# A chunked recurrence on one NeuronCore: scores by quarter array and masked by chunk instead of whole 128-squares

## What is computed

```
def step(S, inp):
    r_t, k_t, v_t, w_t, kk_t, a_t = inp
    sa = einsum('bhvk,bhk->bhv', S, -kk_t)
    S = S * w_t + sa[..., None] * (kk_t * a_t) + v_t[..., None] * k_t
    y = einsum('bhvk,bhk->bhv', S, r_t)
    return S, y
_, y = lax.scan(step, S0, xs)          # 1024 steps, one state per head
```

## Time and profile before

| what | value |
|---|---|
| median of the three timed executions | 2477.08 us |
| the three | 2471.67, 2477.08, 2477.37 us |
| the profiled execution: its own time | 2472.17 us |
| its span, first to last instruction | 2470.4 us |
| mean granted TensorE clock | 0.995 |
| groups in the recurrence | 16 (4 pairs of 4) |
| from one group's first score matmul to the next one's | 39.8 us |

### The profile page before, as it was taken

One profiled execution on the slowest core, in us unless ns is written; L12 is line 12 of the kernel. 1 busy time (PEld: TensorE's weight loads), 2 busy tenths in 40 slices (PEclk: granted clock), 3 DMA queues, 4 the chain that ended last, 5 costly groups with the idle time before them and its releaser, 6 DMA issues.

```text
span 2470.4 us, 33707 instructions
## 1 busy us (share of the span) xinstructions
PE 2376.4 (96%) x12944; PEld 1918.5 (78%) x12944; DVE 1303.9 (53%) x1480; ACT 697.3 (28%) x1103; POOL 773.1 (31%) x416
## 2 busy tenths in 40 slices
PE   5999999999999999998999999999999999999997
PEld 3788878887887788787877788888878787777775
DVE  6553353426342643565638744554451287757766
ACT  3412222223221321433215211111122454214441
POOL 1311131123112313112455433333334445422154
PEclk9999999999999999999999999999999999999998
DMA  3211111121112113663443311111114343211123
GB/s 120 69 52 52 70 51 52 52 69 51 53 50 69 51 52 116 204 203 127 172 150 122 101 42 51 43 50 43 50 53 135 126 120 104 73 61 36 35 77 111
DMA packets 61904, 205.22 MB, mean 83 GB/s; under 512 B 6240, under 2 KB 10464, under 8 KB 61152
## 3 DMA queue, kind: packets, MB, share of 16 engines
q1 hardware_dynamic: 40560, 138.76, 18.0%
q10 hardware_dynamic: 21232, 64.80, 7.2%
HBM read 167.36 MB, written 36.18 MB: 82 GB/s over the span
## 4 chain that ended last, share of the span: by engine, by line
PE 81%; DVE 11%; ACT 3%; DVEq 3%; issue 2%; ACTq 0%; DMA 0%; POOL 0%; POOLq 0%
PE psg L458 9%; PE psg L454 9%; PE psg L459 9%; PE psg L587 5%; PE psg L585 5%; PE psg L580 5%; PE psa L677 1%; PE psg L1125 1%; PE psg L1118 1%; PE psg L1123 1%; PE psb L666 1%; PE psg L1168 1%; PE psg L1162 1%; PE psg L1166 1%; PE psb L673 1%
## 5 line engine op out<-in xcount | busy, mean ns | idle before, releaser
L390 POOL CAST whi<-wraw 128x1024 fp32r<-128x1024 f32 (+1 forms) x176 | 183.1, 1040 | 1471.5 <-PE psg L580 558.2
L392 POOL TENSOR_TENSOR wlo<-wraw,whi 128x1024 fp32r<-128x1024 f32 (+1 forms) x176 | 461.4, 2621 | 27.4 <-issue 6.3
L458 PE MATMUL psg<-xlo,whi 128*128 128x512 f32 x1008 | 400.9, 398 | 0.0
L454 PE MATMUL psg<-xhi,whi 128*128 128x512 f32 x1008 | 398.3, 395 | 2.2 <-issue 1.8
L459 PE MATMUL psg<-xhi,wlo 128*128 128x512 f32 x1008 | 396.9, 394 | 0.0
L585 PE MATMUL psg<-xlo,whi 128*128 128x512 f32 x640 | 260.4, 407 | 0.0
L587 PE MATMUL psg<-xhi,wlo 128*128 128x512 f32 x640 | 260.2, 407 | 0.0
L580 PE MATMUL psg<-xhi,whi 128*128 128x512 f32 x640 | 258.1, 403 | 0.0
L454 PEld LDWEIGHTS psg<-xhi,whi 128*128 128x128 f32 x1008 | 189.2, 188 | 51.9 <-issue 3.2
L458 PEld LDWEIGHTS psg<-xlo,whi 128*128 128x128 f32 x1008 | 189.2, 188 | 45.4 <-issue 0.7
L459 PEld LDWEIGHTS psg<-xhi,wlo 128*128 128x128 f32 x1008 | 189.2, 188 | 44.8
(11 more groups left out here) (595 smaller groups left out, 4815.0 us busy)
## 6 DMA issues: line engine op xcount, KB each, us to landing
wraw<-w SPq DMA_DIRECT2D x224, 512.0 KB, 3.5
later_scratch<-stage ACTq DMA_DIRECT2D x40, 512.0 KB, 2.6
xres<-xt ACTq DMA_DIRECT2D x4, 1024.0 KB, 10.8
RV<-later_scratch SPq DMA_DIRECT2D x4, 1024.0 KB, 12.0
RG<-later_scratch SPq DMA_DIRECT2D x4, 1024.0 KB, 6.3
later_scratch<-rstage ACTq DMA_DIRECT2D x8, 512.0 KB, 2.6
mgr<-later_scratch ACTq DMA_DIRECT2D x8, 512.0 KB, 3.6
mgt<-later_scratch ACTq DMA_DIRECT2D x8, 512.0 KB, 4.6
```

What stands on the lines that cost most here:

```text
L390: pool.tensor_copy(whi[:, u, 0:width], wraw[:, u, 0:width])
L392: pool.tensor_tensor(wlo[:, u, 0:width], wraw[:, u, 0:width], whi[:, u, 0:width].bitcast(F32), ALU.subtract).then_inc(w_ready, 1)
L454: mm = pe.matmul(ps[:, cols], whi[:, slot, w_cols], rhs_hi(k, cols), start=(k == 0), stop=False)
L458: pe.matmul(ps[:, cols], whi[:, slot, w_cols], rhs_lo(k, cols), start=False, stop=False)
```

## The change

The scores are computed by chunk. For each square and each of the two key tiles, four matmuls with 64 rows (head h), 64 weight columns (the keys of chunk c) and 128 streamed columns (the same chunk c of the two query-side tiles) write to partitions 64c to 64c+63 of the head's bank. Head and chunk together choose a quarter of the 128x128 array. The order of the quarters is (0,0), (1,1), (0,1), (1,0), first for `KK`, then for `K`; `scores` is raised by the last two of each square. The off-diagonal blocks are not computed. The mask multiplications are done by chunk as well, two of 64x256 in place of one of 128x512, and no longer write the off-diagonal blocks, which stay as they were set at the beginning. The first group also increments `go` after its wait.

```diff
+        HALVES = [slice(c * CH, c * CH + CH) for c in range(2)]
...
                 pe.wait_ge(sem("rw_prep"), i + 1)
+                pe.sem_inc(go, 1)
                 for g in range(GROUPS):
...
                     for tt in range(2):
                         tl = 2 * g + tt
-                        for h in range(2):
-                            rows = slice(h * CH, h * CH + CH)
-                            kr = KR[rows, tl, :, :].rearrange("p a b -> p (a b)")
-                            pe.matmul(bank[2 * tt + h][:, 0:256], KK[rows, tl * P:tl * P + P], kr,
-                                      start=True, stop=True)
-                            pe.matmul(bank[2 * tt + h][:, 256:512], K[rows, tl * P:tl * P + P], kr,
-                                      start=True, stop=True).then_inc(sem("scores"), 1)
+                        for src, first in ((KK, 0), (K, 256)):
+                            for h, c in ((0, 0), (1, 1), (0, 1), (1, 0)):
+                                rows, chunk = HALVES[h], HALVES[c]
+                                out = bank[2 * tt + h][chunk, first:first + 256].rearrange("p (a b) -> p a b", a=2)
+                                mm = pe.matmul(out[:, :, chunk], src[rows, tl * P + c * CH:tl * P + c * CH + CH],
+                                               KR[rows, tl, :, chunk], start=True, stop=True)
+                                if first and h != c:
+                                    mm.then_inc(sem("scores"), 1)
...
-                    msk = mat[:, M_STRICT:M_STRICT + 2, :].rearrange("p a b -> p (a b)").unsqueeze(1
-                                                                                    ).broadcast_to([P, 2, 256])
                     for q in range(4):
                         v.wait_ge(sem("scores"), 16 * i + 4 * g + q + 1)
-                        tt(SC[:, q, :].rearrange("p (a x) -> p a x", a=2)[:, :, 0:256],
-                           bank[q].rearrange("p (a x) -> p a x", a=2), msk, MUL).then_inc(sem("sc_out"), 1)
+                        for chunk in HALVES:
+                            msk = mat[chunk, M_STRICT:M_STRICT + 2, chunk].unsqueeze(1).broadcast_to([CH, 2, 2, CH])
+                            mm = tt(SC[chunk, q, :].rearrange("p (a x b) -> p a x b", a=2, b=P)[:, :, 0:2, chunk],
+                                    bank[q][chunk, :].rearrange("p (a x b) -> p a x b", a=2, x=2)[:, :, :, chunk],
+                                    msk, MUL)
+                        mm.then_inc(sem("sc_out"), 1)
```

## The result

| | before | changed |
|---|---|---|
| median | 2474.32 us (5 executions, 2471.67 to 2477.37) | 2485.45 us (5 executions, 2483.79 to 2487.33) |
| profiled execution | 2472.17 us | 2487.33 us |
| one group's first score to the next one's | 39.80 us | 40.51 us |
| first score to L653 (now L657) | 6.62 us | 7.33 us |

The ratio of the changed kernel to the one before is 1.0045, with a 95% interval of 1.0034 to 1.0056: slower by 0.45%, or 11.1 us between the medians. The forecast was 2486, a loss of 9.4 us against a kernel before of 2477; with all five executions counted that kernel stands at 2474.32.

What follows compares the result with a forecast made beforehand. The chain scores, VectorE masks, L1404, copies, ScalarE, L653 was taken to bound each group. 16 x (0.99 - 0.42) + 0.3 = 9.4 us on a median of 2477.1 gave 2486 us, range 2474 to 2494.

Steps and rivals of the forecast that it cites:

- Scores, four quarters at once: Score matmuls on TensorE: all four quarters run together, first mask's operand complete after 0.70 us; gain 0.42 us a group.
- The rival of two at a time: Score matmuls: only two quarters run at a time, gain 0.01 us a group; 2493 us, chance 0.18.
- Masks: VectorE: eight half masks at 0.435 us each, 3.48 instead of 2.49; cost 0.99 us a group.
- The overlap rival: VectorE: changing halves does not hold half masks, chain changes by -0.04 us a group; 2477 us, chance 0.10.
- reckoned break-even: Half masks on VectorE: at steps of 0.356 us the chain is as long as before, below it faster.
- It, the copies and ScalarE are unchanged: Chain after the last mask: L1404 still comes 0.09 us later; it, the copies and ScalarE cost nothing extra.
- The limit of 0.38 a group: At L653: fills would let it start only 0.38 us earlier; used in the faster rival, 2471 us, chance 0.04.
- The increment of `go`: Extra semaphore step once a pair, at TensorE's wait for L1395: 0 to 0.1 us each, 0.3 us taken in all.
- A slip in the chances: Chance that the time stays the same, within 0.3%: summed from 0.15 + 0.10 + 0.02, given as 0.26.
- costed nothing for the clock: TensorE's new idle stretches stay well below the 1.5 us at L629, where mean granted clock was 0.995; no cost.

Runs made afterwards that it cites:

- the control: The kernel before with one fill matmul moved from level 1 to ahead of L653; median 2471.33 us, ratio 0.9984.

## Why the prediction was right

**The reading that carried it** was that VectorE's chain and not TensorE's work sets a group. The two half changes show it in both directions: the scores alone give 0.44 a group, the masks alone take 1.17, and in all six kernels without moved fills the period is the time from first score to L653 plus 33.17 to 33.19.

**How much of the hit is luck.** The forecast of 2486 lies 0.5 us from the measured 2485.45, closer than its terms. Its loss was 1.7 us too small (9.4 against 11.1), and the median that it started from 2.8 too high (2477.1, against 2474.3 with all five executions). The two errors nearly cancel.

**Scores, four quarters at once: right.** Forecast 0.70 from the first score to the operands of the first mask, and the mask at 0.7 to 0.75; measured 0.72. In the trace of the changed kernel the 8 records of `KK` for a square stand in 167.81 to 168.26 and those of `K` start 0.27 after the first of them; from there on eight records start every 0.21 to 0.22, two on each quarter. The rival of two at a time, with 1.13, is out. The gain was 0.44 and not 0.42.

The rule that the Trainium skill states in TensorE: Matmul & The Clock Gate, Part 3, The mechanism, that weight loads overlap matmuls in flight only on another row group, doesn't hold here. Two quarters share each row group, and each keeps one matmul record per 0.11 us. That is half of the 0.21 in which 256 columns stream, so no time is left in which a load could stand alone.

**Masks: right in mechanism, 0.04 short.** Forecast 8 x 0.435 = 3.48, measured 3.52; steps with a semaphore check between them are 0.46, those without 0.43. The overlap rival falls with these steps; the run in the other order shows the overlap where no half changes. Its reckoned break-even, steps of 0.356, can be read off that run too: 2.97 for eight, that is steps of (2.97 - 0.42)/7 = 0.36, with no delayed copy, and the kernel came out level with the one before.

**The missed term.** "It, the copies and ScalarE are unchanged" is the sentence that failed: the first copy starts 0.73 after L1404 instead of 0.61, since the last half mask left VectorE's PSUM reads in the upper half. 16 x 0.12 = 1.9 us. It is the largest part of the difference between the 9.1 that the forecast had for the 16 groups and their 11.4. The forecast had looked at the partition half from mask to mask and not on to the next instruction that reads PSUM.

**The limit of 0.38 a group** ("all a group can win on this path") was wrong, though it entered only a rival. It held TensorE's own time ahead of L653 fixed, while the same change shortens it.

**The increment of `go`**: the wait at the first score matmul goes from 5.8 us in four to 6.2, 0.1 each. Forecast 0.3, measured 0.4. Every run with the increment also has the quarter scores (6.2 in all), and the two without either (the half masks with old scores, and the control) have 5.8, so the 0.4 is not separated from what the quarter matmuls do at their start.

**A slip in the chances**: 0.15 + 0.10 + 0.02 for "same" is 0.27 and not 0.26; nothing rests on it.

**What stays open.** The profiled executions differ by 15.2 us, more than the medians. 11.2 of it lie between the first and the last group's start, and 3.4 beyond the recurrence, where both kernels do the same. The cause of the 3.4 is not shown. A layout of the bank in which both chunks' blocks share the same 256 columns, so that one mask of 128x256 would do, was not tried.

## What to carry to other kernels

Where an engine's queue is on the critical path, splitting an instruction by partitions can cost more than the smaller size saves: here two masks of 64x256 take 0.88 us of the queue, and 0.68 even without a change of half, where one of 128x512 takes 0.60. Leave the saving on the engine that gains by it (four quarters of the array) and keep the follow-up whole; if halves must be used, order them so that the half changes as rarely as possible, and look at the next reader of the same memory too. And an engine's saved time has to be given something to do: here three matmuls a group, moved into the gap, were worth as much again as the quarter scores that made the gap (0.49 us and 0.44 of the period), and the clock did not fall in the recurrence of the two quarter-score kernels that had them.

## What was not expected of the hardware

**The start partition of the last read is remembered across an instruction.** Shown above: 0.73 against 0.61 with L1404 in between, 0.72 with the half masks and old scores, 0.61 in the other order.

**Idle time at the start of a pair, and the clock.** The stretches of 4 us around the start of pairs 2 and 3, first in the changed kernel, then in the one before; columns are the length, PE, PEld, DVE, ACT and POOL busy (x), the granted clock, DMA share and GB/s:

```profile
365.50:369.50 4.00, 3.22 (x42) 3.01 (x43) 3.01 (x8) 0.00 (x0) 0.00 (x0) 0.70 0.00 0
604.00:608.00 4.00, 3.39 (x43) 3.03 (x44) 3.05 (x8) 0.00 (x0) 0.00 (x0) 0.76 0.00 0
```

```profile
362.50:366.50 4.00, 3.75 (x29) 3.25 (x30) 2.69 (x6) 0.00 (x0) 0.00 (x0) 1.00 0.00 0
598.00:602.00 4.00, 3.67 (x28) 3.21 (x29) 2.76 (x5) 0.00 (x0) 0.00 (x0) 1.00 0.00 0
```

In the changed kernel the clock falls there from 2.4 to 1.2 GHz for part of the stretch; before, it doesn't. TensorE had stood still for 1.55 us ahead of the scores (1.46 before) and stood still again for 0.52 at L642 (not at all before). The prediction costed nothing for the clock because all single waits stay at or below 1.5 us. In the changed kernel it cost little: the transposes and fills at half speed ran in time that was idle anyway, and only once was L653 late by it, 7.49 instead of 7.33.

In three of the experiments it cost more. The profiled executions of the quarter scores with whole masks, of the masks in another order and of the copies in another order each have one such fall, in the first group of a pair, and L653 comes 1.1 to 1.2 us late there (7.28, 7.76 and 7.23 instead of 6.18, 6.66 and 6.06). The quarter scores with whole masks, in 4 us that begin 1.4 after the first score (127.62), and L653 (here L657) of that group:

```profile
129.00:133.00 4.00, 3.92 (x15) 3.59 (x16) 3.85 (x9) 1.08 (x3) 0.00 (x0) 0.57 0.00 0
134.90 1.00 PE L657 MATMUL psa<-rw_VT,rw_SC 128*128 128x64 f32 x8
```

It waits for nothing but TensorE's own queue: in this group TensorE is the longer chain. Of the nine profiled kernels, the four that have quarter scores and leave the saved time idle show a fall in the recurrence, and the five others (old scores, or fills in the gap) show none. That is one execution each, and even in the changed kernel only two of the four pairs are hit, so what exactly lets the clock fall is not shown.

The clock also goes with the scatter between executions. Of those of the kernel before that ran beside the first experiments, the ones with a mean granted clock of 0.995 or 0.996 took 2471.1 to 2473.4 us, and those with 0.992 took 2477.3. A difference of 0.2% between two single executions is no difference; the period of a group, which repeats to a few hundredths of a microsecond wherever the clock does not fall, tells more.
